# Window-cache copies of a decoder step: issued earlier, and described as 16 KB packets with four leading rows

## What is computed

```
h = rmsnorm(x); z = h @ w_in            # 17 pieces of 512 columns: x, gate, q, k, v, two merge gates
A = (rglru(causal_conv(x part)) * gelu(gate)) @ w_br_lru
B = combine(3 groups of dilated window attention) @ w_br_att
x += (sigmoid(g_lru)*A + sigmoid(g_att)*B) @ w_out
x += moe(rmsnorm(x))                    # top 4 of 32 experts; each expert: 12 MB of weights
x += sigmoid(rmsnorm(x) @ w_ple_gate) * (p @ w_ple)
# also returned, for each of 8 sample rows and 3 groups of 128, 512 and 1024 cached rows:
kv_new = concat(cache[1:], new row)     # the window moved on by one row (one row: 4 KB of k and v)
```

## Time and profile before

| | us |
|---|---|
| median of the runs | 1379.47 |
| the profiled execution, its own time | 1383.31 |
| its span, to which all times of the trace refer | 1381.5 |
| TensorE busy in the span | 1324.8 (96%) |
| DMA engines, mean busy share of 16 | 94% |
| the last weight of the expert stream and what follows it | from about 1345 to 1381.5 |

### The profile page before, as it was taken

One profiled execution on the slowest core, in us unless ns is written; L12 is line 12 of the kernel. 1 busy time (PEld: TensorE's weight loads), 2 busy tenths in 40 slices (PEclk: granted clock), 3 DMA queues, 4 the chain that ended last, 5 costly groups with the idle time before them and its releaser, 6 DMA issues.

```text
span 1381.5 us, 15635 instructions
## 1 busy us (share of the span) xinstructions
PE 1324.8 (96%) x6626; PEld 673.6 (49%) x6626; DVE 371.3 (27%) x524; ACT 218.5 (16%) x401; POOL 17.2 (1%) x33
## 2 busy tenths in 40 slices
PE   7999999999989999999999999999999999999987
PEld 6787788888863333333333333333333233333336
DVE  3069714321231222122121122212222122121223
ACT  3312046323021101101101010110000000001021
POOL 0000111000000000000000000000000000000000
PEclk9999999999999999999999999999999999999999
DMA  9889994888999999999999999999999999999960
GB/s 389 316 278 399 329 385 173 248 320 330 398 372 406 428 427 428 427 428 428 428 427 428 427 429 427 428 427 426 428 429 429 428 428 429 427 429 428 426 296 33
DMA packets 50857, 530.63 MB, mean 384 GB/s; under 512 B 6109, under 2 KB 6253, under 8 KB 22069
## 3 DMA queue, kind: packets, MB, share of 16 engines
q1 hardware_dynamic: 35540, 470.42, 81.7%
q10 hardware_dynamic: 13841, 54.68, 10.6%
q0 software_dynamic: 1424, 4.76, 1.6%
HBM read 525.08 MB, written 58.38 MB: 422 GB/s over the span
## 4 chain that ended last, share of the span: by engine, by line
PE 65%; DMA 23%; ACTq 5%; DVE 3%; ACT 3%; issue 1%; SPq 0%; POOL 0%; DVEq 0%
PE PS L868 34%; DMA ring<-in_wexp 15%; PE PS L597 14%; DMA Zb<-in_wexp 5%; ACTq L421 5%; PE PS L923 3%; PE PS L884 3%; DMA ring<-in_w_ple_gate 2%; PE PS L1052 2%; PE PS L905 2%; DVE ring L1385 1%; PE PS L875 1%; ACT Zb L1262 1%; PE PS L676 1%; PE PS L611 1%; DMA cst<-in_cst 1%
## 5 line engine op out<-in xcount | busy, mean ns | idle before, releaser
L868 PE MATMUL PS<-ring,Zb 128*64 128x512 f32 x2304 | 517.1, 599 | 15.6 <-DMA ring<-in_wexp 13.3
L868 PEld LDWEIGHTS PS<-ring,Zb 128*64 128x64 f32 x2304 | 160.6, 138 | 331.4 <-issue 298.5
L597 PE MATMUL PS<-HL,ring 128*128 128x264 f32 x1024 | 233.9, 388 | 0.0
L597 PEld LDWEIGHTS PS<-HL,ring 128*128 128x128 f32 x1024 | 194.2, 191 | 33.1 <-issue 0.4
L1630 DVE COPY attT<-PS 64x512 f32<-64x512 f32 x32 | 21.9, 683 | 325.2 <-PE PS L868 325.2
L1270 ACT ACTIVATE Zb<-Zb 128x512 f32<-128x512 f32 x32 | 20.2, 630 | 450.3 <-DVE Zb L1610 450.3
L868 PE MATMUL PS<-Zb 128*64 128x512 f32 x392 | 88.9, 595 | 1.3 <-DMA Zb<-in_wexp 1.3
L868 PE MATMUL PS<-HL,Zb 128*64 128x512 f32 x368 | 83.5, 596 | 2.7 <-DMA HL<-in_wexp 2.7
L1600 DVE TENSOR_TENSOR xc<-xc,PS 128x528 f32<-128x528 f32 x64 | 44.8, 700 | 109.9 <-PE PS L923 107.9
L1262 ACT ACTIVATE Zb<-PS 128x512 f32<-128x512 f32 x32 | 19.1, 597 | 329.5 <-PE PS L890 329.5
L923 PE MATMUL PS<-Zb,attT 128*128 128x264 f32 x240 | 71.1, 416 | 0.0
(11 more groups left out here) (244 smaller groups left out, 879.4 us busy)
## 6 DMA issues: line engine op xcount, KB each, us to landing
ring<-in_wexp SPq DMA_DIRECT2D x144, 2048.0 KB, 28.3
Zb<-in_wexp SPq DMA_DIRECT2D x24, 2048.0 KB, 30.3
HL<-in_wexp SPq DMA_DIRECT2D x23, 2048.0 KB, 27.6
ring<-in_win SPq DMA_DIRECT2D x16, 2048.0 KB, 11.9
out_kvs<-in_cache ACTq DMA_DIRECT2D x8, 4032.0 KB, 32.6
out_kvs<-in_cache ACTq DMA_DIRECT2D x8, 1984.0 KB, 22.1
ring<-in_kt SPq DMA_DIRECT2D x2, 2048.0 KB, 16.4
ring<-in_vt SPq DMA_DIRECT2D x2, 2048.0 KB, 10.8
```

Of the source, the lines that this page charges most:

```text
L597: last = mm(PS[:, z_bank(n), 0:T], w[:, k, t * P:(t + 1) * P], hT[:, k, :], start=(k == 0), stop=(k == KT - 1))
L868: last = mm(PS[CAP * h:CAP * (h + 1), bank, :], src[:, k, f:f + CAP], part(k, h) if alone else w[:, k, h * CH:(h + 1) * CH], start=(not se ...
```

## The change

Three things change. The description of a copy: the leading dimension goes from 16 to 4, and four rows that lie next to each other become one run of 16 KB. The places of the copies in ScalarE's program: the large copies 0, 4, 5 and 6 and the last pair move forward. And SP asks for `w_ple` and `pT` right behind the split slot. No line of TensorE, VectorE or GpSimd changes.

```diff
         def shift(eng, g, b):
 
             n = (WB[g] - 1) // 16 * 16
-            eng.dma_start(a[f"kvs{g}"][b, 0:n, :].rearrange("(r q) n -> q r n", q=16),
-                          a[f"cache{g}"][b, 1:n + 1, :].rearrange("(r q) n -> q r n", q=16)).then_inc(S.kv_copy, 16)
+            eng.dma_start(a[f"kvs{g}"][b, 0:n, :].rearrange("(r q k) n -> q r (k n)", q=4, k=4),
+                          a[f"cache{g}"][b, 1:n + 1, :].rearrange("(r q k) n -> q r (k n)", q=4, k=4)).then_inc(S.kv_copy, 16)
...
             for view, n0, n1 in parts:
                 sp.dma_start(view, weights(0, 4)[:, n0 * CH:n1 * CH]).then_inc(S.w_part, 16)
+            sp.dma_start(wpl, a["w_ple"].rearrange("(k p) n -> p k n", p=P)).then_inc(S.wpl_in, 16)
+            sp.dma_start(pT, a["pT"]).then_inc(S.wpl_in, 16)
             sp.wait_ge(S.wo_mm, KT)
             general(0, 5)
             general(1, 0)
...
             general(1, 2)
-            sp.dma_start(wpl, a["w_ple"].rearrange("(k p) n -> p k n", p=P)).then_inc(S.wpl_in, 16)
-            sp.dma_start(pT, a["pT"]).then_inc(S.wpl_in, 16)
...
             evacs(12, 14)
+            shift(act, 2, 0)
             qk_roots(0)
             evacs(14, 16)
-            shift(act, 2, 0)
             evacs(16, 20)
...
             evacs(40, 44)
+            shift(act, 2, 4)
...
                 A(dst, PS[:, 4 + n % 3, 0:T], ACT.Sigmoid, bias=feat[:, j, c:c + 1]).then_inc(S.gate_ev, 1)
+            shift(act, 2, 5)
             rows_out(1)
...
-                if it in (2, 6):
-                    both(it // 4 + 6)
-                if it == 4:
-                    shift(act, 2, 4)
+                if it in (2, 4):
+                    both(it // 2 + 5)
+                if it == 6:
+                    shift(act, 2, 6)
             act.wait_ge(S.z_evac, NZ)
             A(Z[:, ZGA:ZGA + KT, :], Z[:, ZGA:ZGA + KT, :], ACT.Sigmoid).then_inc(S.sig_z, 1)
-            for b in (5, 6, 7):
-                shift(act, 2, b)
+            shift(act, 2, 7)
             for g in range(NG):
                 shift_rest(act, g)
```

## The result

The change takes **1694.88 us** (median of 4 runs, 1691.52 to 1696.98) against 1382.23 us before on the same chip (the three runs of the table above and one more): ratio **1.225**, interval [1.222, 1.228]. Forecast were 1704 us, 1665 to 1820, slower. The profiled execution has a span of 1689.7 us, 308.2 more than before, and its own time is 1691.52 us.

What follows compares the result with a forecast made beforehand. The prediction took DMA engine time as the bound: 1381.5 us span, plus 367 for copies on four engines, minus 43 idle time filled, gives 1705.5, less 2 for the measured time: 1704 us, range 1665 to 1820.

Steps and rivals of the forecast that it cites:

- How a copy is spread: Cache copies' queue: 491 closing packets show engines follow the leading dimension, so 4 leading rows use four engines.
- rival "not the same four": Cache copies: each takes four engines, but varying ones, so load evens out; 1360 to 1385 us, chance 0.03.
- Price of a packet: Cache copies: a 16 KB packet takes 0.63 us (0.612 to 0.702), so 509 us on each of the four.
- The account that decides: Whole kernel: span is the busiest DMA engine's busy plus idle time; before, 1299 us busy and 82 us idle.
- one microsecond of transfer more or less per engine in that time is one microsecond of the end: From 330 to 1345 us: DMA share 1.00, no engine idle, so added or saved transfer time moves the end equally.
- 43 us for idle time: Before 330 us: the four engines fill nearly all of 45 us idle time, -43 us (0 to -45).
- cross-check: Stage before the experts: copies and loads finish at about 690 us; experts start between 575 and 690 instead of 414.
- "0 us" for asking sooner: Copies placed earlier in ScalarE's program: on four engines the slack is gone anyway, so 0 us.
- "0" for `w_ple`: w_ple and pT behind the split slot on SP: same bytes, engines full, 0 us, bounds -3 and +3.
- Rival "16 engines": Cache copies: they still use 16 engines, 18 us less plus 22 us slack filled; 1350 us, chance 0.08.
- Rival "run dry": Before the experts: ScalarE's waits leave the four without queued copies, overlap lost; about 1800 to 1850, at most 1890, chance 0.12.

Runs made afterwards that it cites:

- places alone: The change with copies described as before (16 leading rows, 4 KB each), keeping the earlier places and w_ple's, against the kernel before: 1378.94 us, ratio 0.998.
- description alone: The kernel before with only its copies described as 4 leading rows with runs of 16 KB, all places as before: 1688.93 us, ratio 1.223.

## Why the prediction was right, and where not

- **How a copy is spread** was read rightly from the packet count: the queue has 3857 packets in the change, 3809 with two leading rows and 7185 with eight, with 24 closing packets for each engine that a copy uses, and 2, 4, 8 and 16 leading rows gave 2185, 1695, 1437 and 1379 us. The rule of the Trainium skill ("DMA: Bandwidth & Descriptors", "Why a DMA increments its semaphore by 16 and not by 1") for the number of engines agrees with these counts. The same section of the Trainium skill says that a DMA from SP or ScalarE that uses fewer than 16 gets the lowest-numbered ones; the row at 640 us agrees in that they are the same each time, and no run shows their numbers. The rival "not the same four" falls.
- **Price of a packet**: 0.63 us forecast, 0.63 measured; 509 us on the four stands.
- **The account that decides, span = busy time of the busiest engine + its idle time**, can be counted. All that is not a copy takes 68.4% of the span in the change (the shares of the queues), and with the rests and bias rows it makes 1160 us on each engine, if it lies evenly on the 16. With 510 us of copies the four are busy for 1670 of 1690 us. By the packet records, counted the same way, the busiest engines have 2179 of 2184 us with two and 1410 of 1431 with eight, and before all 16 have 1300 of 1382. (Times of packets that overlap are counted twice in this, so the idle time is somewhat more than the difference.) So in the change the waits on ScalarE are no cause beside the engines: on the four hardly any idle time is left for one. Four-engine copies issued from a program that nothing waits for were not tried; by this count they could win back no more than some tens of the 308 us. The two runs with two samples on four engines have the same 1402 us of work on the four, and 58 us idle with the first two, 29 with the last.
- **Which step failed: "one microsecond of transfer more or less per engine in that time is one microsecond of the end".** That was read from a share of 1.00 from 330 us on, and it is wrong from 330 to 450 us. The engines were full there, but with copies that nothing waited for; without any copy the time is the same (no copies, 1.000), and with most of the copies moved ahead of that stretch it falls by 3 us (places alone). The loads were held by slots, and these by TensorE, not by engines. From 450 us on the statement was not tried.
- **Why the sum came out all the same.** The prediction took off 142 us for before's copies and 43 us for idle time, 185 in all, and the run without copies has 185 us of free engine time. These are two parts of one quantity, the engine time that loads leave free, and the sum holds whether the loads wait for engines or for slots. That the wrong reading did no harm is luck of this question: asked for better copies, it promised 22 us where 3 came. By the quantity, 1384 + 509 - 185 = 1708 us of span; measured 1689.7. With eight engines 1384 + 254 - 185 = 1453, measured 1430.6; with two 2217, measured 2183.9; with 16, 127 is under 185 and nothing shows. The account is 18 to 33 us high each time. Packets whose times overlap would do that, and they do overlap: up to 722 us, when the last packet of a copy ended, the four have 510 us of copies and, by the packet records, 245 of loads, 33 us more than there are; the prediction had 13. That a share above 1 is the overlap of two queues is too narrow: without copies the share from 990 to 1310 us is 1.01 as well.
- **The cross-check was too early**: experts between 575 and 690 us, measured 707.9. It let them start when ScalarE gets its last issue in and took the rest of the queue as work beside the experts. In fact the rests waited 115 us, to 678.5 us, and the last packet of a copy ended at 722 us. So the stretch at half the rate of 428 GB/s, which was to follow, hardly exists.
- **"0 us" for asking sooner** held on four engines: the change has a ratio of 1.225 [1.222, 1.228], the description alone 1.223 [1.221, 1.225], and no difference is shown. "0" for `w_ple` held in the kernel before.
- **Rival "16 engines"**: its condition did not come true, but its price can be judged, 1340 to 1358 us: the places alone on 16 engines give 1379. The same failed step.
- **Rival "run dry"** was right about the mechanism and wrong about when: it is what the first two samples on four engines do, 74 us lost for 234 - 185 = 49 by the account. In the change the queue stayed supplied: by the packet records at least 100 packets of earlier copies stood ahead on each of the four at every issue from 88 to 563 us.

## What to carry to other kernels

Before asking what a copy's packets are like, ask over how many DMA engines its description spreads: the leading dimension said it here, and the closing packets of a queue count it. A full DMA share does not say that transfers are the limit; leave out the ones that nothing waits for, and see whether the time moves. And a copy that nobody waits for can still stop the engine that asks for it, with all that stands behind in its program: whether its cover holds is decided near the place where the queue fills, not over the whole program.

## What the runs showed of the hardware

- An issue on ScalarE's queue waits when enough packets of earlier copies stand ahead on an engine. By the packet records, before, one went through in 0.8 us with 126 ahead, and the next waited at 189 until 112 were left. In the change, and with eight engines, a copy that waited went through at about 120, with two engines mostly at about 70. So it is not one number of packets, and no run settles what it is. The three large copies of the earlier trace rows, 63 packets each on an engine, are as many bytes on four engines as on 16, but a copy of 63 packets drains in 40 us (0.63 each) instead of 11 (0.176).
- The wait is not that queue's alone: with the four engines full, SP's issues for the split slot, `w_ple` and `pT` took 4 to 27 us on its own queue, where before they took 0.3 to 0.7. One SP issue behind large loads of its own took 7.5 us even without copies.
- An engine moved 27 GB/s of DRAM to DRAM copies (108 GB/s on four from 310 to 330 us), as much as it moves of weights (428 on 16).
- While TensorE had nothing to do, from 620 to 680 us (and from 310 to 330), its granted clock was 0.50, the lower of its levels (1.2 GHz); over the span 0.905. A matmul of z took 396 ns on average for 388 before, 7 us in all, and TensorE was busy 31 us longer over the span (1356.2 for 1324.8). Whether the end feels any of it, no run shows.
